# Second norm's sums of squares: full-width products in two banks, or four column strips in one bank with a picking block that adds and spreads them

## What is computed

```
def rmsnorm(x, g):
    y = x * rsqrt(mean(x * x, axis=-1) + RMS_EPS)
    return y * g
x = x + gt1 * (merged @ w_out)
h2 = rmsnorm(x, g_norm[1]) * (1 + sc2) + sh2
u, gg = split(h2 @ w_ffn_in, 2)
x = x + gt2 * ((silu(gg) * u) @ w_ffn_out)
```

## Time and profile before

| | |
|---|---|
| median of 3 runs | 1026.42 us (1024.86 to 1027.81) |
| the profiled execution's own time | 1028.69 us |
| its span, first to last instruction | 1026.9 us |
| mean granted TensorE clock | 0.992 of full |
| TensorE busy | 987.2 us (96%) |
| VectorE, ScalarE, GpSimd busy | 614.5, 480.4, 349.1 us |

### The profile page before, as it was taken

The page is one execution under the profiler, slowest core; times in us unless marked ns, Lnnn a source line. Parts: engine busy times, 40 slices in busy tenths (PEclk is TensorE's granted clock), DMA queues, the critical chain, the costliest instruction groups (busy, mean ns, idle before and its releaser), DMA issues.

```text
span 1026.9 us, 27048 instructions
## 1 busy us (share of the span) xinstructions
PE 987.2 (96%) x10868; PEld 902.3 (88%) x10868; DVE 614.5 (60%) x1344; ACT 480.4 (47%) x1084; POOL 349.1 (34%) x337
## 2 busy tenths in 40 slices
PE   6999999999999999898999999999999999999996
PEld 4898888999997676666798999999999999999996
DVE  4985565594036666665448566888888887800003
ACT  4565555463453554445242255555555555711113
POOL 1156432153314260601170455332332332133330
PEclk9999999999999999999899999999999999999998
DMA  9957676484201000020342632224324333233322
GB/s 354 392 172 265 206 254 233 154 264 135 100 34 50 14 13 24 14 86 4 128 134 73 220 95 72 83 82 117 88 82 121 84 83 96 68 103 85 84 57 88
DMA packets 118760, 123.45 MB, mean 120 GB/s; under 512 B 5428, under 2 KB 102880, under 8 KB 116232
## 3 DMA queue, kind: packets, MB, share of 16 engines
q1 hardware_dynamic: 113440, 112.97, 34.3%
q10 hardware_dynamic: 5224, 9.10, 2.6%
HBM read 109.45 MB, written 15.23 MB: 121 GB/s over the span
## 4 chain that ended last, share of the span: by engine, by line
PE 84%; DVE 7%; ACT 4%; issue 3%; POOL 1%; ACTq 1%; DVEq 0%; POOLq 0%
PE ps L2230 48%; PE ps L2902 22%; PE ps L2428 11%; PE ps L2643 1%; DVE s_sb L1808 1%; PE ps L2543 1%; DVE hl L1499 1%; DVE Pb L1779 1%; ACT x_sq L933 1%; POOL w_lo L736 0%; DVE XX L1789 0%; PE ps L2935 0%; POOL w_lo L901 0%; ACTq L919 0%; DVE rbx L1512 0%
## 5 line engine op out<-in xcount | busy, mean ns | idle before, releaser
L895 POOL TENSOR_TENSOR ws_lo<-w_raw,ws_hi 128x512 fp32r<-128x512 f32 x63 | 80.5, 1293 | 146.3 <-DVE ps L2062 132.6
L2230 PE MATMUL ps<-hh,w_hi 128*128 128x274 f32 x512 | 108.4, 295 | 1.5 <-DVE hl L1499 0.7
L2230 PE MATMUL ps<-hl,w_hi 128*128 128x274 f32 x512 | 106.1, 290 | 1.0 <-DVE al L2144 1.0
L2230 PE MATMUL ps<-hh,w_lo 128*128 128x274 f32 x512 | 106.1, 290 | 0.0
L736 POOL TENSOR_TENSOR w_lo<-w_raw,w_hi 128x2048 fp32r<-128x2048 f32 x11 | 50.8, 4622 | 140.3 <-ACT w_hi L943 123.4
L2902 PE MATMUL ps<-th,ws_hi 128*128 128x274 f32 x336 | 97.5, 290 | 0.0
L2902 PE MATMUL ps<-tl,ws_hi 128*128 128x274 f32 x336 | 97.4, 290 | 0.0
L2902 PE MATMUL ps<-th,ws_lo 128*128 128x274 f32 x336 | 97.1, 289 | 0.0
L2230 PEld LDWEIGHTS ps<-hh,w_hi 128*128 128x128 f32 x512 | 81.0, 189 | 7.6 <-issue 5.7
L2230 PEld LDWEIGHTS ps<-hl,w_hi 128*128 128x128 f32 x512 | 80.8, 189 | 1.2 <-DVE al L2144 1.2
L2230 PEld LDWEIGHTS ps<-hh,w_lo 128*128 128x128 f32 x512 | 80.9, 190 | 0.8 <-issue 0.8
(11 more groups left out here) (495 smaller groups left out, 2868.9 us busy)
## 6 DMA issues: line engine op xcount, KB each, us to landing
w_raw<-in_w_ffn_in SPq DMA_DIRECT2D x44, 512.0 KB, 5.0
w_raw<-in_w_in SPq DMA_DIRECT2D x42, 512.0 KB, 5.9
ada_l<-in_w_ada SPq DMA_DIRECT2D x16, 1024.0 KB, 5.2
ada_w<-in_w_ada SPq DMA_DIRECT2D x8, 1024.0 KB, 13.5
w_raw<-in_w_ffn_out SPq DMA_DIRECT2D x16, 384.0 KB, 4.0
w_raw<-in_w_ffn_out SPq DMA_DIRECT2D x16, 320.0 KB, 3.3
g_d<-gst SPq DMA_DIRECT2D x16, 274.0 KB, 2.6
gring<-g_d SPq DMA_DIRECT2D x16, 274.0 KB, 4.2
```

The source lines that it names most:

```text
L895: pool.tensor_tensor(slot_of(ws_lo, p), block_source(s, p), slot_of(ws_hi, p).bitcast(F32), ALU.subtract) .then_inc(wslo_done, 1)
L2230: return pe.matmul(out, lhsT, rhs, start=start, stop=stop)
```

## The change

The 8 tiles' sums go to four strips of 32 output rows in bank 4 alone: tile k, half h goes to strip j = 2*(k%2) + h, with a 128x32 block of ones. So even and odd tiles have strips of their own. Behind the last sum VectorE copies the bank (128x274) into SBUF (`ss_part`), and TensorE, ahead of k = 4 of U_UP, makes two fp32 products of 128x128 by 128x274 with a block `pick`, whose ones stand in the rows of the strips of one half. They add even and odd strips, 32 equal rows each, and give the result to all 128 rows, in banks 4 and 5 as before; the mean divides by 32*D. VectorE waits for that between the copy and L2044. GpSimd makes `pick` by five memsets behind the low parts of U_WO. The new counts go on semaphores that were used earlier (x0_in, c_in).

```diff
@@ SBUF
+        pick, ss_part = at("pick", [P, 2, P], E + 13088), at("ss_part", [P, H], E + 14112)
@@ GpSimd
             for i in range(U_WO, U_UP + 1):
                 low_in_four(i, i % 2)
+                if i == U_WO:
+                    link(pool.memset(pick[:, :, :], 0.0))
+                    for j in range(4):
+                        strip = pool.memset(pick[32 * j:32 * j + 32, j % 2, :], 1.0)
+                    link(strip)
@@ VectorE
             dve.wait_ge(ss_mm, KD)
-            link(sts(halves(rstd2[:, :]), pair(2), 1.0 / D, RMS_EPS, ALU.mult, ALU.add))
+            dve.tensor_copy(ss_part[:, :], ps[:, 4, 0:H]).then_inc(ss_read, 1)
+            dve.wait_ge(ss_spread, SS_SPREAD + 1)
+            link(sts(halves(rstd2[:, :]), pair(2), 1.0 / (32 * D), RMS_EPS, ALU.mult, ALU.add))
             dve.reciprocal(rstd2[:, :], rstd2[:, :]).then_inc(var_ready, 1)
@@ TensorE
                 pe.wait_ge(sq_done, KS + k + 1)
                 for h in range(2):
-                    ins = mm(ps[:, 4 + h, 0:H], ones[:, :], sq_a[:, k % 2, h * H:(h + 1) * H], k == 0, k == KD - 1)
+                    j = 2 * (k % 2) + h
+                    ins = mm(ps[32 * j:32 * j + 32, 4, 0:H], ones[:, 0:32], sq_a[:, k % 2, h * H:(h + 1) * H], k < 2, k >= KD - 2)
                 ins.then_inc(ss_mm, 1)
+
+            def spread_square():
+
+                pe.wait_ge(ss_read, SS_READ + 1)
+                for h in range(2):
+                    ins = mm(ps[:, 4 + h, 0:H], pick[:, h, :], ss_part[:, :])
+                ins.then_inc(ss_spread, 1)
@@ TensorE, U_UP
             for k in range(KD):
                 if k == 2:
                     sum_square(KD - 1)
+                if k == 4:
+                    spread_square()
                 pe.wait_ge(h2_done, k + 1)
```

More of the change, by code:

```diff
@@ L346, in build @@
         PTS, PTH, PTL = KS, 1, KS
+        ss_read, ss_spread, SS_READ, SS_SPREAD = x0_in, c_in, 16 + 3 * 10, 32 + 4 * 10
         v_back, V_BACK = vtok_out, 16 * KS
```

## The result

The changed kernel took 1029.03 us (median of 22) beside 1025.93 us for the kernel before (22): ratio 1.0026, 95% interval 1.0016 to 1.0036, so **2.7 us slower, 1.6 to 3.7**. (The two medians alone lie 3.1 apart; the 2.7 is the ratio times the time of before.) Measured again later (8 executions beside 27) it came to 1.0045, interval 1.0033 to 1.0057, 4.6 us slower. Both say slower.

What follows compares the result with a forecast made beforehand. TensorE, busy 96% of the span, was taken as the bound, with VectorE's chain arriving almost together. Late restart +2.7 and clock +1.5 made +4.2 us on the 1026.42 median, rounded up to 1030.7 us; range 1027.9 to 1032.5, the forecast's own 1029.7 to 1031.7.

Steps and rivals of the forecast that it cites:

- The bound: End of U_UP: VectorE's chain and TensorE arrive almost together; a mean later by more than 0.19 us makes TensorE wait.
- Strips: Sums of squares: four strips run at once, a batch of two sums costing 0.78 us instead of 1.84.
- The earlier gain: Before U_UP: it starts 0.70 us earlier, bound by tile 7's residual, plus 0.2 from ScalarE's squares waiting less.
- The late mean: VectorE's mean after the spread at k = 4 starts 2.9 us later; TensorE's restart by sevens comes 2.7 later.
- the signs: Trace places: U_UP near 633, mean near 641, restart by sevens near 650 after about 3 us waiting, half clock behind 633 or 650.
- The later stage: Units by sevens: they give none of the 2.7 us back; the later stall at 657 may grow a little.
- nothing gives this back: Units by sevens: engines hand work back and forth without long pause, so the 2.7 us delay stays.
- The clock: Two sparse TensorE stretches, before U_UP and before the restart: one fall to half clock that costs, 1.5 us (ends 0 and 3.3).
- No clock loss: Rival, both TensorE pauses: no fall costs, only the late mean is left, +2.7 us, 1029.1; chance 0.30.
- Both pauses cost: Rival, both TensorE pauses: half clock costs behind each, +2.7 + 3.3 = +6.0 us, 1032.4; chance 0.13.
- Strips one after another: Rival, the sums: one bank's four strips do not overlap, restart 3.8 us late, 1030.2, no first pause; chance 0.07.
- faster by TensorE's list: Rival, sums and restart: TensorE's shorter list alone decides, -2.7 us, 1023.7; chance 0.04.

Runs made afterwards that it cites:

- experiment 6: Changed kernel with the sums of tiles 0 to 5 cut to 16 of 274 columns and left out of the result: +3.9 us against the kernel before.
- experiment 4: Changed kernel with 15 ordinary products into an unread bank filling TensorE's pause before U_UP: +2.8 us, again +3.7 us, against the kernel before.
- experiment 2: Changed kernel with full-width sums instead of strips, copy and spread kept: +3.6 us (+2.1 to +5.2) against the kernel before.
- experiments 2 to 4: Besides experiment 2 and experiment 4: changed kernel with the two spreading products one tile earlier (k == 3, not k == 4), +1.1 us against the kernel before.
- experiments 1 and 6: Besides experiment 6: changed kernel with strips kept, copy, its wait and the spreading products left out: -1.5 us (-3.3 to +0.2) against the kernel before.
- the mended order: Changed kernel, spread at k == 3 into banks 6 and 7, two weight sums during VectorE's wait: +0.9, again +0.1 us against before; first pause filled: -0.8, again -1.4.

## Why the prediction was right, and where not

*The bound.* Right. VectorE's chain to the line that frees banks 0 and 1 and TensorE's list arrived together, and a later mean came out as waiting: 0.35 became 3.11 in the weight load's row of 648.01 below.

*Strips.* Right. Four strips of one bank do run at once: the batch at 613.08 takes 614.04 - 613.08 = 0.96 us to the second ordinary pair, less 0.26 is 0.70, where I had 0.78 and full width takes 1.84; sum 7 takes 635.12 - 634.17 = 0.95, less 0.26 is 0.69, where I had 0.78. That is 1.84 / 0.70 = 2.6 times as fast. The Trainium skill (TensorE: Matmul & The Clock Gate, Measured speedup vs the span model) has 2.38 for three column tiles; the trace agrees in kind, with 2.6 for four. By that page's model, which the prediction took up, four strips take about the time of one; one product costs 0.46 at full width here (0.93 / 2), and the batch on four strips took 0.70, going in and out of strips included, so the model is not reached. But the batch on four strips cost what a lone sum on two did (0.70 and 0.69): the second pair came free.

*The earlier gain.* Right in kind: U_UP starts with the residual of tile 7, which experiment 6 shows. The size was 30.90 - 29.77 = 1.13, where I had 0.70 + 0.2. The residual ends 30.15 behind the first sum in before and 629.33 - 599.66 = 29.67 after, so 0.48 earlier, not 0.2. Most of that, 0.4, comes in one cycle of ScalarE's work, from one `th` (the high part of the token sums, made once for two tiles) to the next. In the kernel before, a square in between waits for a sum:
```profile
614.90 1.12 ACT L1328 ACTIVATE th<-tq 128x1096 fp32r<-128x1096 f32 x1 [4.49 <-DVE tq L2028]
...
618.12 0.66 ACT L1324 ACTIVATE sq_a<-xT 128x548 f32<-128x548 f32 x1 [0.30 <-PE ps L2230]
...
627.56 1.12 ACT L1328 ACTIVATE th<-tq 128x1096 fp32r<-128x1096 f32 x1 [4.82 <-DVE tq L2028]
```
and in the changed one it doesn't:
```profile
611.60 1.12 ACT L1336 ACTIVATE th<-tq 128x1096 fp32r<-128x1096 f32 x1 [4.49 <-DVE tq L2036]
...
614.43 0.65 ACT L1332 ACTIVATE sq_a<-xT 128x548 f32<-128x548 f32 x1
...
623.86 1.12 ACT L1336 ACTIVATE th<-tq 128x1096 fp32r<-128x1096 f32 x1 [4.48 <-DVE tq L2036]
```
From one `th` to the next it is 12.66 us there and 12.26 here.

*The late mean.* I had 2.9 later and the restart 2.7; measured at full clock (experiment 4) 2.6 and 2.3. The difference is the earlier start, just named. In the places that I gave for the signs, which are those of the first profile of before (3.22 later), the changed profile's mean is at 642.3 and its restart at 651.2, for "near 641" and "near 650": the half clock came ahead of both, and I had counted its price apart from them.

*The later stage.* I said that nothing gives it back. First it grew by 0.3, as I allowed: the second wait of the units by sevens went from 0.51 us in the kernel before
```profile
657.16 0.19 PEld L2902 LDWEIGHTS ps<-hh,ws_hi 128*128 128x128 f32 x1 [0.51 <-DVE ws_lo L2069]
...
668.17 0.19 PEld L2902 LDWEIGHTS ps<-hh,ws_hi 128*128 128x128 f32 x1 [0.23 <-DVE ws_lo L2069]
```
to 0.81:
```profile
648.01 0.19 PEld L2922 LDWEIGHTS ps<-hh,ws_hi 128*128 128x128 f32 x1 [3.11 <-DVE ff_g L2096]
...
658.04 0.19 PEld L2922 LDWEIGHTS ps<-hh,ws_hi 128*128 128x128 f32 x1 [0.81 <-DVE ws_lo L2079]
...
669.05 0.19 PEld L2922 LDWEIGHTS ps<-hh,ws_hi 128*128 128x128 f32 x1 [0.27 <-DVE ws_lo L2079]
...
854.85 0.19 PEld L2922 LDWEIGHTS ps<-hh,ws_hi 128*128 128x128 f32 x1 [0.17 <-DVE ws_lo L2079]
```
From the restart to the third unit's first product it is 668.17 - 647.43 = 20.74 before and 669.05 - 648.01 = 21.04 after. But the 17 units from 669.05 to 854.85 take 185.80 us, and 186.35 and 186.29 in the two profiles of before. Here the step "nothing gives this back" failed, by 0.5 us. It is not the change's idea that wins it: all twelve profiles of the changed kernel and its edits, also those with an early mean, lie between 185.80 and 185.92. What in the edited programs makes a unit 0.03 us shorter stays open; no run was made for it.

*The clock.* The sum at full clock is 2.3 + 0.3 - 0.5 = +2.1 us. On top I put 1.5 for one fall in every execution. The size is right for the first pause, 1.45. It is wrong for the second: from the restart to that same product full clock takes the 21.04 just given, and with half clock behind the restart it is 21.65 (experiment 2, 669.97 - 648.32), so a fall there costs 0.6: the slower products use up the wait of 0.81 for VectorE ahead of the second unit, which has no wait in experiment 2, and only what goes beyond it is lost. And it doesn't come every time: 3.2 between the means of all executions, less 2.1 (the traces) or 1.7 (the executions at 0.997 or more), leaves 1.1 to 1.5 us on average, the fall elsewhere in the kernel included, where I had 1.5 for each. The size of this term was about right; what I missed is that it comes and goes. The forecast and what was measured: **+4.3 forecast; +2.7 and +4.6 in two measurements, +3.2 between the means of all executions**. The forecast's own range, 1029.7 to 1031.7, holds the second measurement (1030.80) but not the first (1029.03), which fell below 1029.5, where I had put 0.31 against 0.64 above. So the mechanism was right, and the size of the whole too large by 1.1 on average: 0.4 at the restart, 0.3 in the later units (0.5 given back, less the 0.2 by which the second wait grew beyond the 0.1 that I had allowed), and the rest, 0.4, in a fall that does not come each time. The rule cited there (the Trainium skill, TensorE: Matmul & The Clock Gate, Loop structure matters more than you think) agrees in kind: the pauses came from the order of the loop's work, and the clock fell behind them.

*The rivals.* "No clock loss" (+2.7) has the first measurement's number but not its content: the real sum at full clock is 2.1. "Both pauses cost" appears in no profile: each of the changed kernel, of experiments 2 to 4 and of experiment 6 shows half clock behind one of the two pauses, none behind both. "Strips one after another" and "faster by TensorE's list" fell, the first by the batches' 0.67 us, the second by experiments 1 and 6.

## What to carry to other kernels

Before taking products out of a full engine, look for the event that starts its next stage: if that is another engine's, what is saved ahead of it turns into waiting, and what is added behind it is paid in full. A reduction cut into two steps with a copy between them puts a round trip on every engine's queue; give the waiting engine work that needs neither (here two weight sums), and put the second step as early as the copy allows. Pauses of 1 to 3 us on TensorE have a second price, the clock, paid in some executions only; judge it over many executions' mean clock, not from one profile, and fill the pause if filling costs nothing.

## What was not expected of the hardware

The two short pauses around sum 6, 0.75 and 1.22 us with 0.66 of work between them, were followed by half clock in six of the seven profiles that had them (in experiment 6 they were 1.40 and 1.37); the mended order had them twice, once with half clock behind them and once without. None of the seven profiles without them, the two of before, experiment 2 and the four with filling, shows half clock at this place. The pause of 2.9 us without any work was followed by half clock in the three profiles whose first pause was absent or filled (experiments 2 and 4), and in none where the first had already cost. The price of such a stretch was about 1.45 us ahead of the late mean, where TensorE's own list decides, and 0.6 where VectorE's does.
